# Two attentions that begin beside the last chunk of their projection

## What is computed

```
for l in range(2):
    m = split(silu(c) @ ada_w[l] + ada_b[l], 6)      # six modulations, for x and for ctx
    h = x * (1 + m[1]) + m[0]                        # both for x and for ctx
    if l == 0:   # 8 + 8 heads of 64
        qa, ka, va, qb, kb, vb = split(h @ ev_w_in)
        qa, ka = rope(rms_norm(qa)), rope(rms_norm(ka))
        y = concat(softmax(qa ka^T) va, softmax(qb kb^T + bias) vb) @ ev_w_out
    else:        # 16 heads, 2 key heads, a window and a sink
        q, k, v = split(h @ od_w_in);  q, k = rope(q), rope(k)
        y = softmax(window(q k^T), sink) v @ od_w_out
    x = layer_norm(ALPHA * x + m[2] * y);  then the same with a convolved, gated FFN
```

## Time and profile before

| | |
|---|---|
| median of 3 runs | 1751.89 us (1751.03 to 1752.73) |
| the profiled execution | 1749.54 us |
| its span, first to last instruction | 1748.2 us |
| TensorE busy | 1612.0 us, 92% |
| VectorE busy | 1052.7 us, 60% |
| ScalarE busy | 805.9 us, 46% |
| GpSimd busy | 239.5 us, 14% |
| share of the chain of waits | TensorE 80%, VectorE 10%, ScalarE 7% |
| mean granted TensorE clock | 0.964 |

### The profile page before, as it was taken

One profiled execution on the slowest core, in us unless ns is written; L12 is line 12 of the kernel. 1 busy time (PEld: TensorE's weight loads), 2 busy tenths in 40 slices (PEclk: granted clock), 3 DMA queues, 4 the chain that ended last, 5 costly groups with the idle time before them and its releaser, 6 DMA issues.

```text
span 1748.2 us, 26862 instructions
## 1 busy us (share of the span) xinstructions
PE 1612.0 (92%) x10834; PEld 1393.1 (80%) x10834; DVE 1052.7 (60%) x1923; ACT 805.9 (46%) x1514; POOL 239.5 (14%) x284
## 2 busy tenths in 40 slices
PE   5899979999998999979899997888999998899997
PEld 3788757877776787867799976777999787689986
DVE  3643855565353534787677757565677666567764
ACT  2322863433232323448455553554555455456553
POOL 1100420011010100013011101142111011321110
PEclk8999999999999999989899998899999998999999
DMA  9457022263563222130345452323455533245551
GB/s 378 166 230 260 10 82 97 82 255 128 209 238 147 97 96 99 49 118 2 138 165 204 171 187 102 137 95 122 157 182 189 188 124 121 73 152 186 184 195 68
DMA packets 39418, 257.27 MB, mean 147 GB/s; under 512 B 5504, under 2 KB 6784, under 8 KB 10496
## 3 DMA queue, kind: packets, MB, share of 16 engines
q1 hardware_dynamic: 36416, 249.61, 39.3%
q0 software_dynamic: 1296, 4.72, 0.8%
q10 hardware_dynamic: 1584, 1.23, 0.2%
HBM read 254.49 MB, written 1.05 MB: 146 GB/s over the span
## 4 chain that ended last, share of the span: by engine, by line
PE 80%; DVE 10%; ACT 7%; issue 2%; DMA 1%; POOL 1%; SPq 0%; ACTq 0%; DVEq 0%
PE ps L461 23%; PE ps L463 22%; PE ps L462 22%; PE ps L477 2%; DVE wl L1651 2%; PE ps L603 2%; PE ps L625 2%; PE ps L612 2%; ACT wh L1230 2%; ACT arena L1563 1%; PE ps L996 1%; PE ps L503 1%; DMA raw<-in_ev_w_in 1%; ACT arena L1301 1%; PE ps L587 1%
## 5 line engine op out<-in xcount | busy, mean ns | idle before, releaser
L1651 DVE TENSOR_TENSOR wl<-raw,wh 128x1024 fp32r<-128x1024 f32 (+1 forms) x330 | 386.4, 1212 | 427.9 <-ACT wh L1230 427.5
L1230 ACT CAST wh<-raw 128x1024 fp32r<-128x1024 f32 (+1 forms) x340 | 335.2, 1035 | 549.9 <-PE ps L463 420.1
L461 PE MATMUL ps<-xh,wh 128*128 128x256 f32 (+1 forms) x1534 | 484.3, 316 | 8.3 <-ACT arena L1520 8.0
L462 PE MATMUL ps<-xl,wh 128*128 128x256 f32 (+1 forms) x1534 | 477.6, 311 | 0.0
L463 PE MATMUL ps<-xh,wl 128*128 128x256 f32 (+1 forms) x1534 | 477.4, 311 | 0.0
L461 PE MATMUL ps<-wh,xh 128*128 128x512 f32 (+2 forms) x876 | 325.3, 371 | 35.5 <-ACT home L1230 10.4
L461 PEld LDWEIGHTS ps<-xh,wh 128*128 128x128 f32 x1534 | 295.2, 192 | 33.5 <-issue 9.5
L462 PE MATMUL ps<-wl,xh 128*128 128x512 f32 (+2 forms) x876 | 319.5, 365 | 0.0
L463 PE MATMUL ps<-wh,xl 128*128 128x512 f32 (+2 forms) x876 | 319.5, 365 | 0.0
L462 PEld LDWEIGHTS ps<-xl,wh 128*128 128x128 f32 x1534 | 295.3, 193 | 16.2 <-issue 1.7
L463 PEld LDWEIGHTS ps<-xh,wl 128*128 128x128 f32 x1534 | 295.2, 192 | 15.4
(11 more groups left out here) (208 smaller groups left out, 1791.1 us busy)
## 6 DMA issues: line engine op xcount, KB each, us to landing
raw<-in_ada SPq DMA_DIRECT2D x48, 1024.0 KB, 6.4
raw<-in_up SPq DMA_DIRECT2D x44, 1024.0 KB, 5.3
raw<-in_fin SPq DMA_DIRECT2D x44, 1024.0 KB, 4.8
raw<-in_down SPq DMA_DIRECT2D x22, 1024.0 KB, 4.8
raw<-in_fout SPq DMA_DIRECT2D x22, 1024.0 KB, 4.8
raw<-in_win SPq DMA_DIRECT2D x12, 1024.0 KB, 4.8
raw<-in_ev_w_in SPq DMA_DIRECT2D x9, 1024.0 KB, 7.7
raw<-in_wout SPq DMA_DIRECT2D x8, 1024.0 KB, 4.9
```

Of the source, the lines that this page charges most:

```text
L461: e.matmul(out, A[0], B[0], start=first, stop=False)
L462: e.matmul(out, A[0], B[1], start=False, stop=False)
L1230: e.copy(hi_of(j)[:, a:b], raw_of(j)[:, a:b]).then_inc(*S.hi.up((j, half)))
L1651: e.tensor_tensor(lo_of(j)[:, a:b], raw_of(j)[:, a:b], hi_of(j)[:, a:b].bitcast(F), ALU.subtract).then_inc(*S.lo.up((j, half)))
```

## The change

Three parts. In `chunk_order` the last two modulation chunks of layer 0 (22 and 23) go ahead of chunk 8 of `ev_w_in`, and TensorE does them between the query and the key transposes. The values of chunk 8 (`vb1`) are computed inside the first attention: tiles 0 and 1 behind `scores(1)`, tiles 2 and 3 behind `scores(2)`, in the banks 7 and 6, with their copies at the same units of ScalarE's and VectorE's programs. And in the second layer each tile is rotated at once (`qk_rest()` in the loop), the queries are turned one chunk earlier, and query chunk 3 is done inside the attention: its product behind `scores(1)`, the turning of query pairs 4 and 5 behind `scores(2)`, of pairs 6 and 7 behind `scores(3)`, all in banks 6 and 7; its rotations and copies are at the same units, and the conversion of the second chunk of `od_w_out` is at unit 4.

```
@@ chunk_order
     for n, i in enumerate((3, 1, 4, 2, 5, 6, 7, 8)):
-        o += ev(i) + ada(0, 8 + 2 * n, 9 + 2 * n)
+        two = ada(0, 8 + 2 * n, 9 + 2 * n)
+        o += two + ev(i) if i == 8 else ev(i) + two
@@ tensor_program: attention1
-                for signal, at in ready if i == 0 else ():
+                for signal, at in ready.get(i, ()):
...
                 if i < A.n:
                     scores(i)
+                    fill(i)
@@ tensor_program: first layer
         head_features("qt", range(4), ...)
+        ada_two()
         head_features("kt", range(2), ...)
-        tokens("ev_w_in", 8, "vb1", t4)
-        ada_two()
         ada_finish(5)
-        for key in [("vb1", 3), ("vb1", 2), ("kt", 1), ("kt", 0)]:
+        for key in [("vb0", 3), ("vb0", 2), ("kt", 1), ("kt", 0), ("qt", 3), ("qt", 2)]:
             q.wait_ge(*copied(key))
+        def last_values(i):
+            for t in {1: (0, 1), 2: (2, 3)}.get(i, ()):
+                nb[0] = t + 1
+                tokens("ev_w_in", 8, "vb1", (t,))
+        span[:] = [6, 2]
+        attention1(ATT["ev"], {0: ..., 18: ...}, last_values)
@@ tensor_program: second layer
-        for i in range(1, 4):
-            od_queries(i)
...
+        od_queries(1)
+        head_features("okt", range(2), ...)
+        od_turned(0)
+        od_queries(2)
+        od_turned(1)
+        for key in [("oqt", 3), ("oqt", 2), ("okt", 1), ("okt", 0)]:
+            q.wait_ge(*copied(key))
+        def last_queries(i):
+            nb[0] = 1
+            if i == 1:
+                od_queries(3)
+            elif i in (2, 3):
+                od_turned(i)
@@ vector_program (scalar_program likewise)
         copies_heads(copy, "qt", range(4), QT0, 512, 0.125)
+        ada_rows(5)
         copies_heads(copy, "kt", range(2), KT, 512)
-        copies_vb(copy, 1)
-        ada_rows(5)
         ada_mods(5)
         def beside(i):
+            copies_vb(copy, 1, {1: (0, 1), 2: (2, 3)}.get(i, ()))
...
-        for n, tiles in enumerate(QK1):
+        for n, tiles in enumerate(QK1[0:5]):
             for tile in tiles:
                 qk(tile)
+            qk_rest()
...
+        def beside_od(i):
+            if i == 1:
+                for tile in QK1[5]:
+                    qk(tile)
+                    qk_rest()
+            elif i in (2, 3):
+                copies_heads(copy, "oqt", [2 * i, 2 * i + 1], QT1, 256, -0.125)
+            elif i == 4:
+                weights(after(J["od_w_in", 3]))
```

More of the change, by code:

```diff
@@ L589, in gates, with attention1 @@
                     free[b] = [(S.act, ("gate", key, grp, half))]
-        def attention1(A, ready):
+        def attention1(A, ready, fill=lambda i: None):
             key = A.key
@@ L835, in tensor_program, with od_turned @@
         od_keys((2, 3), ("f1", 1))
-        for i in range(1, 4):
-            od_queries(i)
-            if i == 1:
[L839 to L850, removed]
+        def od_turned(i):
+            head_features("oqt", [2 * i, 2 * i + 1], lambda t, j: QS1[:, t, 128 * j:128 * j + 128], t2,
+                          [(S.vec, ("oqk", (2 if i == 0 else 4 + 2 * i) + 1))])
+        od_queries(1)
+        head_features("okt", range(2), lambda t, j: KS[:, t, j, :, :].rearrange("p two d -> p (two d)"), t4, [(S.vec, ("oqk", 5))])
+        od_turned(0)
[5 more added lines that the diff above has]
+            nb[0] = 1
+            if i == 1:
+                od_queries(3)
+            elif i in (2, 3):
+                od_turned(i)
+        span[:] = [6, 2]
+        attention1(ATT["od"], {0: [(S.ea, ("ova", 3))], 8: [(S.ea if SIDE.get(("oqt", j)) == "act" else S.ev, ("oqt", j)) for j in (4, 5)],
+                               12: [(S.ea if SIDE.get(("oqt", j)) == "act" else S.ev, ("oqt", j)) for j in (6, 7)]}, last_queries)
+        span[:] = [0, 6]
         mixed("od", "od_w_out", 1, (1, 2))
@@ L1150, in copies_kb, with copies_vb @@
             copy(k, KTB[:, 2 * i + f, :], ps[BANK.get(k, 0)][:, 0:512], (S.proj, k))
-    def copies_vb(copy, i):
-        for t in t4:
+    def copies_vb(copy, i, tiles=range(4)):
+        for t in tiles:
             k = (f"vb{i}", t)
@@ L2131, in vector_program @@
                 weights(after(J["od_w_in", i]))
-            if n >= 2:
+            if n >= 1:
                 next(spare, None)
@@ L2135, in vector_program @@
                 copies_heads(copy, "okt", range(2), KT, 512)
[L2136 to L2139, removed]
-            copies_heads(copy, "oqt", [2 * i, 2 * i + 1], QT1, 256, -0.125, free)
-        diagonals = gates(1, 2, 1)
-        attention1(ATT["od"], lambda i: next(diagonals) if i in (6, 8) else None)
+            if n >= 3:
+                copies_heads(copy, "oqt", [2 * (n - 3), 2 * (n - 3) + 1], QT1, 256, -0.125, free)
+        next(spare, None)
+        diagonals = gates(1, 2, 1)
+        def beside_od(i):
+            if i == 1:
+                for tile in QK1[5]:
+                    qk(tile)
+                    qk_rest()
+            elif i in (2, 3):
+                copies_heads(copy, "oqt", [2 * i, 2 * i + 1], QT1, 256, -0.125)
+            elif i == 4:
+                weights(after(J["od_w_in", 3]))
+            elif i in (6, 8):
+                next(diagonals)
+        attention1(ATT["od"], beside_od)
         fold(3, 1, 4, 3, 2, ("f1", 1))
```

14 lines of the change are left out of this document (7 added, 7 removed).

## The result

The changed kernel takes **1757.37 us** in the median (1752.96 to 1760.33, 10 runs); the kernel before, run beside it, 1750.43 us. The ratio is 1.0034, with a 95% interval of 1.0024 to 1.0043: slower by 6 us (4 to 7.5). The profiled execution took 1758.29 us, 8.75 more than that of before, with a span of 1757.0 us.

A forecast was written before the change was run, and what follows sets the result against it. Both attentions were taken as bound by TensorE once running, with gains only at their starts and the first's second half. +4.8 (first attention) and +3.5 (second) gave +8.3 us: 1757.8 profiled, 1760.2 median, range 1753.5 to 1766.5.

The forecast's parts named there:

- the wait for the bank: Second attention, ahead of the fifth scores: TensorE idles 3.9 us until ScalarE copies query pair 4 out of bank 6.
- First attention, +4.8 forecast: Chunk 8's late load holds up the copies queued behind its cast; fifth scores at 178.05 instead of 173.24.
- the lower of the two bounds: Chunk 8's load in flight: 5.5 us taken, with 4.9 and 7.7 as bounds.
- The 3.9 us that I had called idle: First attention before the change, first to fifth scores: 9.2 us pass with 5.25 us of TensorE work.
- Second attention up to the fifth scores, 0 forecast: First scores 6.8 us earlier, but fifth scores at 783.1 against 783.16 before.
- Behind the fifth scores, +3.5 forecast: Second attention: two uncovered waits, +0.9 for the first values product and +2.6 for the od_w_out split.
- The od_w_out split: Converting the od_w_out chunk in unit 4 of the second attention costs at least a half chunk's waits in the first: +2.6.
- The wait of the first values product: Second attention: this product waits for bank 6 until pair 6 is copied, behind the fourth group's exponentials: +0.9 us.
- sign of being wrong that I had set: Second attention: if waits in units 3 to 7 sum to under 3 us, the second half of the sum falls.
- Rival (a): Both attentions: chunk 8's load is not late; -3.9 in the first, up to -3 in the second; median 1745.0; chance 0.12.
- rival (b): First attention as forecast, the second gains 3 us: +1.8, 1753.7; chance 0.13.
- (c): Both attentions at upper bounds, +7.0 and +6, or the clock falls again after the 3.9 us idle: 1765; chance 0.15.

The follow-up runs named there:

- the old load order: The changed kernel with chunk 8 of ev_w_in again loaded ahead of modulation chunks 22 and 23: 1749.57 us, 0.9988 of the kernel before.
- the second part's second execution: Second profiled execution (1746.54 us) of the kernel before with only the second layer's part of the change; that repeat's median 1749.45 us, ratio 0.9989.

## Why the prediction was right

It forecast 1760.2 us and slower; 1757.37 came. The mechanism was right in the first attention. In the second the wait for the bank was, the low clock was left out, and the sum came out because errors cancelled. Point by point:

**First attention, +4.8 forecast, +4.3 measured; right in its mechanism.** The load was issued 1.14 us after modulation chunk 20, as worked out. It landed 4.9 us later, not 5.5: the lower of the two bounds was right. (The Trainium skill's 6.15 us for 1 MB, in "DMA: Bandwidth & Descriptors", Bandwidth, would have been 1.2 us too long here; that row is for a load that GpSimd issues, and this one is SyncE's.) The wait was 5.45 us where 6.3 stood, the modulation chunks took 2.94 us where 3.5 stood. The 3.9 us that I had called idle ahead of the fifth scores of before were 2.5 of waiting and 1.4 of low clock (TensorE is busy 6.69 of the 9.18 us, at 0.81, with 5.25 us of work); the work put there took up both, so the term held. That the cost is what queues behind the cast is shown by the kernel that moves only the cast (8.6 us less). Of the Trainium skill's rule to issue early, compute, and wait late ("DMA: Bandwidth & Descriptors", Rules for kernel authors), the second half bears out here more than the first: once nothing stood behind the wait, the late issue cost 0.84 us.

**TensorE-bound from the fifth scores on: right.** The third stretch is 80.56 to 80.60 us in before, the change and the old load order. It is 81.3 to 81.4 in three other profiles, one of them with the code of before there, where the clock fell once.

**Second attention up to the fifth scores, 0 forecast, +0.95 measured** (51.41 + 19.35 against 58.48 + 11.33). First scores 7.1 us sooner (6.8 forecast), bank wait 3.46 us (3.9 forecast), released by the copy of pair 4 as named. What failed is the clock: I let it stay up behind this wait and held its fall for a rival's bound. In the profiled execution it fell, in another of the same code it did not (then -0.8).

**Behind the fifth scores, +3.5 forecast, +3.4 measured, but not by the terms given.** The od_w_out split, forecast +2.6, was 1.06 + 0.64 = 1.7 us of waits (1.9 in the second part's second execution), and 0.76 of that comes back if it is moved to unit 17. The wait of the first values product, forecast +0.9, was 0.35 at full clock, and hidden at the low clock. The rest of the 3.4, 1.7 us, was the low clock: TensorE is busy 46.11 us there for 44.40. The sum held because two terms were too high and one was left out, and that is luck. By the sign of being wrong that I had set (waits in units 3 to 7 under 3 us) this half stands, 3.46 + 1.06 + 0.64 = 5.2, but by the wait for the bank; around the conversion I had expected 2 to 3 and 1.7 came.

**The time.** The profiled executions differ by 8.75 us, for 8.3 forecast, with 0.1 of it outside of the stages only because larger differences there cancel; the medians differ by 6.9. I added the 2.35 us between before's profiled execution and its median to the forecast: the changed kernel's profiled execution was above its median, so this step put 1760.2 where 1757.8 stood. Rival (a) fell with the cast at 152.89, rival (b) with the bank wait; (c)'s fall of the clock came, without its bounds.

## What to carry to other kernels

When a load moves later in a queue, ask which instruction waits for it and what stands behind that instruction: the lateness cost 0.8 us, the copies queued behind the cast 7.3, of which 2.3 were the low clock that the wait brought. Work filled into an attention's start needs its copies ahead of the exponentials, not behind them, where they hold PSUM banks. And when a part's time contradicts its stage in the trace, profile it again before you explain it: one execution of a kernel can be 7 us off another.

## What the runs showed of the hardware

The same wait of 3.46 us at the same place was followed by a granted clock of 0.62 over the next 8 us in one execution and of 1.00 in another of the same kernel, with the same 84 matmuls ahead of it. What differed was the clock ahead of the wait. In the one, the low clock that began before the first scores lasted until 5.9 us after them, and these matmuls took 13.37 us; in the other it lasted until 4.1 us after them, and they took 12.62. The same goes for all seven profiles that have this wait: in the five in which the clock fell behind it, the low clock had lasted until 5.3 to 5.9 us after the first scores, in the two in which it did not, until 4.0 to 4.1. That goes together; that it is the cause is not shown. A wait of 1.97 us was followed by a fall in one kernel and one of 1.98 us at the same place was not in the next. So what the clock does behind a short wait is not settled by the length of the wait; it is worth 2.8 us here. Over a whole execution these falls differ by 10 us of TensorE time, and two edits whose changed stages add up within 0.2 us have times that do not add up.
